# Attention of a two-layer hybrid backbone: TensorE multiplies with discarded results at the end of the preparation and in the first unit

## The reference

```python
# B, grouped-query, per block of 128 queries
s = einsum('bqkgd,bskd->bkgqs', qi, k) * (HEAD_DIM ** -0.5)
p = softmax(s, axis=-1)
out = einsum('bkgqs,bskd->bqkgd', p, v)
# C, differential
p = softmax(einsum('bqhmd,bshmd->bhmqs', qi, k) * (DIFF_HD ** -0.5), axis=-1)
a = p[:, :, 0] - lam * p[:, :, 1]
out = einsum('bhqs,bshe->bqhe', a, v)
```

## Time and profile before

| | |
|---|---|
| median of 3 runs | 2790.07 us |
| profiled execution | 2791.23 us |
| its span, first to last instruction | 2789.6 us |
| mean granted TensorE clock | 0.924 |
| PE busy | 2423.0 us, 87% of the span |
| VectorE (DVE) busy | 1459.6 us, 52% |
| ScalarE (ACT) busy | 1069.0 us, 38% |
| GpSimd (POOL) busy | 313.0 us, 11% |
| attention, preparation, layer 0 | about 412 to 444 us |
| attention, main stage, layer 0 | about 445 to 638 us |
| attention, main stage, layer 1 | about 1605 to 1804 us |

### The profile page before, as it was taken

The page is one execution under the profiler, slowest core; times in us unless marked ns, Lnnn a source line. Parts: engine busy times, 40 slices in busy tenths (PEclk is TensorE's granted clock), DMA queues, the critical chain, the costliest instruction groups (busy, mean ns, idle before and its releaser), DMA issues. The chain is left out here.

```text
span 2789.6 us, 47165 instructions
## 1 busy us (share of the span) xinstructions
PE 2423.0 (87%) x19308; PEld 2202.9 (79%) x19308; DVE 1459.6 (52%) x2079; ACT 1069.0 (38%) x1752; POOL 313.0 (11%) x334
## 2 busy tenths in 40 slices
PE   5996778978899999989948698794899999999993
PEld 4984555778899999989836567794799999999992
DVE  5576555685422222246656747642454555455556
ACT  4331235673421122143212456621444444344443
POOL 0055233000000000000643220001000000000002
PEclk8998897999999999989979979895899999999996
DMA  5233656503122322213157000012865676676654
GB/s 210 85 82 72 198 184 214 175 1 91 51 73 66 92 64 69 66 52 92 32 116 206 23 1 1 24 38 76 257 205 166 209 233 200 185 217 211 194 182 173
DMA packets 453116, 340.49 MB, mean 122 GB/s; under 512 B 90961, under 2 KB 421151, under 8 KB 451935
## 3 DMA queue, kind: packets, MB, share of 16 engines
q1 hardware_dynamic: 436383, 277.43, 34.4%
q10 hardware_dynamic: 11520, 41.95, 4.7%
q0 software_dynamic: 5056, 18.88, 1.8%
HBM read 287.68 MB, written 50.53 MB: 121 GB/s over the span
## 5 line engine op out<-in xcount | busy, mean ns | idle before, releaser
L2359 PE MATMUL ps<-h_hi,w_hi 128*128 128x256 f32 x1408 | 400.2, 284 | 5.5 <-DVE w_lo L2442 5.5
L2359 PE MATMUL ps<-h_lo,w_hi 128*128 128x256 f32 x1408 | 399.6, 284 | 0.0
L2359 PE MATMUL ps<-h_hi,w_lo 128*128 128x256 f32 x1408 | 399.6, 284 | 0.0
L2442 DVE TENSOR_TENSOR w_lo<-w_raw,w_hi 128x2048 fp32r<-128x2048 f32 (+1 forms) x180 | 309.2, 1756 | 120.6 <-ACT w_hi L2392 120.6
L2359 PEld LDWEIGHTS ps<-h_hi,w_hi 128*128 128x128 f32 x1408 | 271.3, 193 | 8.7 <-issue 5.9
L2359 PEld LDWEIGHTS ps<-h_lo,w_hi 128*128 128x128 f32 x1408 | 271.4, 193 | 2.8
L2359 PEld LDWEIGHTS ps<-h_hi,w_lo 128*128 128x128 f32 x1408 | 271.2, 193 | 0.0
L2392 ACT CAST w_hi<-w_raw 128x2048 fp32r<-128x2048 f32 (+1 forms) x180 | 256.5, 1473 | 2.6 <-DMA w_raw<-in_moe_w_down 2.6
L2661 PE MATMUL ps<-ffn_h_hi,w_hi_ffn 128*128 128x320 f32 x704 | 161.5, 311 | 5.5 <-DVE ffn_h_lo L378 4.2
L2661 PE MATMUL ps<-ffn_h_lo,w_hi_ffn 128*128 128x320 f32 x704 | 161.3, 310 | 0.0
L2661 PE MATMUL ps<-ffn_h_hi,w_lo_ffn 128*128 128x320 f32 x704 | 161.2, 310 | 0.0
(11 more groups left out here) (426 smaller groups left out, 5610.4 us busy)
## 6 DMA issues: line engine op xcount, KB each, us to landing
w_raw<-in_moe_w_gu SPq DMA_DIRECT2D x182, 512.0 KB
w_raw<-in_moe_w_down SPq DMA_DIRECT2D x91, 512.0 KB
G_decay<-in_ada_w ACTq DMA_DIRECT2D x54, 512.0 KB, 4.7
w_ahead<-in_ffn_w_gu SPq DMA_DIRECT2D x44, 512.0 KB, 5.3
slots_h<-tm SPq DMA_DIRECT2D x13, 1024.0 KB, 11.1
slots_y<-tm SPq DMA_DIRECT2D x12, 1024.0 KB, 11.2
w_ahead<-in_ffn_w_down SPq DMA_DIRECT2D x16, 704.0 KB, 4.7
oA<-in_ada_w ACTq DMA_DIRECT2D x20, 512.0 KB, 5.1
```

What stands on the lines that cost most here:

```text
L2359: mm = pe.matmul(ps[:, j % 2, half * BLK:(half + 1) * BLK], gu(wt, j, half, k), x[:, k, :], start=(k == 0 and n == 0), stop=(k == KC - 1 a ...
L2442: dve.tensor_tensor(wlo[:, q, part], raw[:, q, part], whi[:, q, part].bitcast(F32), ALU.subtract).then_inc(s["lo_d" if down else "lo_u"], 1)
```

## The change

A helper issues `n` multiplies, each with 128 columns of `qB` as weights and 512 columns of `qB` as moving operand, into PSUM bank `b`. Their results are read by nobody: bank 7 is unused in the preparation, bank 4 in step -1, and bank 7 in step 0 until the first weighted values, which overwrite it. It is called with 12 after the last transposes of the preparation, with 8, 4 and 4 in step -1 (after score tiles 2, 3 and 4) and with 3, 3 and 3 in step 0 (after the first, second and third `turn`; the third behind score tile 2 of unit 1). That makes 37 in each of the two layers. Nothing waits for them and they wait for nothing; nothing is removed or moved.

```diff
--- before.py
+++ after.py
@@ -1476,6 +1476,11 @@
                     what, t = item
                     return P * (1 + t) if what == "cache" else 0 if t == 0 else P + PAST + (t - 1) * P
 
+                def keep_running(pe, b, n):
+
+                    for _ in range(n):
+                        pe.matmul(ps[:, b, :], qB[:, 1, 0:P], qB[:, 0, 0:512], start=True, stop=True)
+
                 C_SCALE = -DHC ** -0.5
                 names = "gain_in lv_in cache_in chain ms ctx_out lsum lexp squared hi lo turned_b turned_c out_b out_c out_ck"
                 with stage(nc, names) as (block, s):
@@ -1612,6 +1617,7 @@
                             for h in range(NC2):
                                 mm = pe.transpose(bank[5 + h // 4][0:RC, h % 4], skC[:, u, h].bitcast(F32), self.ident)
                             mm.then_inc(s["turned_c"], 1)
+                        keep_running(pe, 7, 12)
 
 
             units = [("B", h, 0) for h in range(HB)] + [("C", h, m) for h in range(HC) for m in range(2)]
@@ -1800,6 +1806,8 @@
                         ahead, now, done = v + 1 < NU, 0 <= v < NU, v >= 1
                         if now:
                             turn(v, 0)
+                        if v == 0:
+                            keep_running(pe, OB, 3)
                         if done:
                             weigh(v - 1, 1, 0)
                             weigh(v - 1, 1, 1)
@@ -1814,6 +1824,10 @@
                             turn(v, 2)
                         if ahead:
                             scores(v + 1, 2)
+                        if v < 0:
+                            keep_running(pe, RING, 8)
+                        if v == 0:
+                            keep_running(pe, OB, 3)
                         if done:
                             weigh(v - 1, 1, 4)
                             weigh(v - 1, 1, 5)
@@ -1825,6 +1839,8 @@
                             weigh(v, 0, 1)
                         if ahead:
                             scores(v + 1, 3)
+                        if v < 0:
+                            keep_running(pe, RING, 4)
                         if now:
                             turn(v, 5)
                             weigh(v, 0, 2)
```

## The result

The changed kernel takes 2776.56 us (median of 7 runs, 2773.34 to 2785.59), the kernel before, run beside it, 2793.21 us (7 runs): ratio 0.9939, 95% interval 0.9919 to 0.9959. The profiled execution took 2776.56 us, its span is 2774.9 us. TensorE's mean granted clock rose from 0.924 to 0.938.

A forecast was written before the change was run, and what follows sets the result against it. TensorE at half clock was taken to bound the first unit. Layer 0: 0.9 - 7.3 - 1.8 = -8.2; layer 1: 0.9 - 7.3 - 2.15 = -8.55; together -16.8, hence 2773.3 us, range 2766 to 2785.

The forecast's parts named there:

- What bounds the stretch: Start of attention's main stage: unit 0 is bound by TensorE at half its clock, 1.2 instead of 2.4 GHz.
- The twelve cost nothing: End of the preparation: twelve multiplies hidden under VectorE's reduction cost nothing; without that cover 2.8 us per layer.
- The clock falls into the first tiles and the eight bring it back: First score tiles: half clock from around 446, full after the block of eight; first mark 0.9 us later per layer.
- the clock never falls: Rival, start of the main stage: full clock survives 1.8 us idle, mark 1.5 us earlier, -21.6, 2768.5 us; chance 0.16.
- Unit 0: First unit of the main stage: at full clock 12.9 instead of 20.19 us, -7.3 us per layer.
- Unit 1: Second unit of the main stage becomes a plain one of 14.69 us: -1.8 in layer 0, -2.15 in layer 1.
- The late return: Rival: full clock only where unit 0 begins, first mark 5.9 us late, together -6.8, 2783.3 us; chance 0.22.
- Slower: Rival: clock stays at half through unit 0 and TensorE carries the extra work, +9.3 per layer, 2809 us; chance 0.06.
- Short falls in other units: Later units of the main stage: short falls of the clock can land otherwise, a microsecond or two either way.

The follow-up runs named there:

- e4: All 37 discarded multiplies per layer in their places, each with 16 columns instead of 512, against the kernel before: ratio 1.0052.
- e8: The changed kernel with 6+6+6 instead of 3+3+3 discarded multiplies in unit 0: one run at 2789.81 us.
- e10: The changed kernel plus 8 discarded multiplies of 256 columns in all C units but the first: 2772.05 us, ratio 0.9912 to the kernel before.
- e2: Only the 8+4+4 between the first score tiles, without the twelve and the nine, against the kernel before: ratio 0.9975.
- e3: Only the 3+3+3 in unit 0, against the kernel before: ratio 0.9954.
- e5: The changed kernel measured and profiled once more, against the kernel before: 2777.66 us, ratio 0.9938.
- e12: The changed kernel plus the C-unit multiplies of e10 and 12 ahead of the output projection: 2772.75 us, ratio 0.991 to the kernel before.
- e7: The changed kernel with 16 instead of 12 ending the preparation, plus 8 and 2 before the cache items' transposes: ratio 0.9943 to the kernel before.
- e11: e10 plus 4 discarded multiplies between score tiles 1 and 2 of unit 0 and 12 ahead of the output projection: ratio 0.992 to the kernel before.
- e1: Only the twelve at the end of the preparation, the other discarded multiplies set to 0, against the kernel before: ratio 1.000.

## Why the prediction was right

Forecast 2773.3 us, 16.8 less than before; measured 2776.56 and 16.7 less than the runs beside it. The absolute time lies 3 us off because those runs of before have a median 3 us above the one I started from. The close agreement is in part luck. The interval of the ratio allows 11 to 23 us and doesn't separate the forecast from the rival's 21.6, and the medians are over runs that probably mix two starts: up to unit 2's end one is worth 10.4 and 10.8 us in the two layers, the other some 7.9 and 8.2, and falls in later units add or take up to 4.5 per layer.

- **What bounds the stretch: shown.** PE is the busiest engine at either clock; e4, with every instruction and few columns, gains nothing; in e8 two thirds of TensorE's added time lengthen unit 0 at full clock.
- **The twelve cost nothing: right, if barely.** They end at 448.34, VectorE's last instruction ends at 448.32; where the twelve ran at full clock, as priced, they ended some 0.7 us before it (e10: 448.67 and 449.41). The preparation was 34.6 and 34.5 us, but e2 and e3, without the twelve, have 34.4 to 34.6 too. The 33.3 of layer 0 before came in no other layer; the shortest elsewhere are 34.0 and 34.1. Transposes at half clock are not the whole of it, since layers whose last transposes ran at full clock took 34.0 to 34.5; what else differed is open.
- **The clock falls into the first tiles and the eight bring it back: one of two cases.** The profile of the changed kernel showed the rival "the clock never falls", with its number: first mark 1.53 us earlier, 1.5 foretold. The reason is another than the rival's: the fall comes earlier, and the twelve at half clock mend it before the stage. Of the five executions seen with this start, two are so in both layers (changed kernel, e5) and three are as forecast in both (e8, e10, e12): first mark 14.22 to 14.28, 1.0 us late where I had 0.9. I gave 0.16 to a number that came in two of five. My evidence for a fall was weak too: I took the wait of 1.75 us before the fall at 1767 for its reason. Layer 0 has the same wait three times, and the clock is 1.00 without a break from 483.6 to 640.5:

```profile
582.42 0.38 PE L1773 MATMUL ps<-p_hi,vC 128*128 128x256 f32 x1 [1.76 <-DVE p_lo L1854]
...
1766.26 0.38 PE L1773 MATMUL ps<-p_hi,vC 128*128 128x256 f32 x1 [1.75 <-DVE p_lo L1854]
```

- **Unit 0: mis-sized.** I had 12.9 us, it is 13.40, and three terms were off. The nine cost 2.4 us, not 2.1: each further multiply of a block costs 0.23, as priced, but each block 0.1 more (0.79 for three, 1.48 for six). The wait on VectorE, for which I left 0.2, is 0.73. The score tiles took 1.36 to 1.45 us, not 1.47, which gives 0.3 back. From the changed kernel:

```profile
460.26 0.94 PE L1482 MATMUL ps<-qB 128*128 128x512 f32 x3
461.05 0.39 PE L1737 MATMUL ps<-kB,qB 128*128 128x512 f32 x1
...
467.21 0.63 PE L1761 MATMUL ps<-cst,tm 128*128 128x128 f32 x4 [0.73 <-DVE p_lo L1872]
```

The 0.1 may be the load at the edge of a block; no run isolates it. Inside a block the loads are hidden. So the rule of the Trainium skill that loads overlap only between different row groups (TensorE: Matmul & The Clock Gate, Part 3, "The mechanism") isn't borne out. The same section also lets a load into a background weight buffer go ahead, and no run here shows whether that is what happens.

- **Unit 1: right.** 14.4 us where I had 14.69, 0.3 better than a plain unit.
- **The late return: real, but not here.** e2 has it, with the first mark 5.9 us late exactly as priced. With all parts in place it was seen once, in layer 0 of e7 (first mark 17.56). Why the eight suffice in one layer and not in another is open; the moment of the fall, which differs between executions, is the likely reason, and no run set it.
- **Slower:** no profile of the changed kernel shows it. In e4, where the clock isn't brought back, the instructions with 16 columns alone cost 2.5 us ahead of the first mark and 0.6 in unit 0. My argument that the clock came back by itself at the end of unit 0 was misread: in the kernel before it came back 4.9 and 5.7 us into unit 1.
- **Short falls in other units: undersized.** I allowed one or two microseconds. The rest of the stage took 131.6 to 136.1 us by how many of them fell in the C units, 4.5 us per layer, and e10 took all of them away.

The rule of the Trainium skill that transposes don't engage the full clock (same page, Part 4) stays contradicted by the earlier trace rows, and with it the extra chance that it would have given the late case.

## What to carry to other kernels

Where TensorE bounds a stretch and the granted clock there is 0.50, multiplies with discarded results can pay, but only where they stand in a wait that exists anyway or make dense what is thin; judge a place by its profile with the part alone, since here one part was worth nothing by itself and another three quarters of the whole. The cheapest are those inside a known wait for another engine, as in e10: there they cost nothing, and in the six layers with them (e10, e11, e12) no single fall was left. And since the moment of a fall differs between executions, take several profiles and look at each layer before naming a cause.

## What was not expected of the hardware

The same gap-free block of eight multiplies of 512 columns brought the clock back in six layers of e8, e10 and e12 and failed in both of e2 and in one of e7. In layer 1 of e1 a full clock fell at the end of a wait of 0.87 us between score tiles, while the 1.76 us of a C unit passed three times in layer 0 of the kernel before without a fall. Multiplies of 16 columns, as many and in the same places, did not bring it back. A kernel with one part of the change (e2) spread its runs over 35 us, twice what the whole change is worth.
